# Second norm's modulations as rows in four quarters of the array, and the context's scale and shift on VectorE

## What is computed

```python
mod = silu(c) @ w_mod + b_mod                 # 6 x 1024, one for the context, one for the latent tokens
sh1, sc1, g1, sh2, sc2, g2 = split(mod, 6)
h = rmsnorm(x, norm1_g) * (1 + sc1) + sh1     # first norm
x = x + g1 * (mixer(h) @ w_o)                 # products "wo"
h = rmsnorm(x, norm2_g) * (1 + sc2) + sh2     # second norm
q = h @ wq                                    # products "wq"
x = x + g2 * peer(q, h)                       # expert retrieval over 16384 experts
y = rmsnorm(x, final_g)
```

## Time and profile before

| | us |
|---|---|
| median of 3 runs | 2236.38 |
| lowest and highest | 2235.76, 2242.87 |
| the profiled execution | 2240.45 |
| its span in the profile | 2238.6 |
| PE busy | 2134.1 (95%) |
| DVE busy | 1626.6 (73%) |
| ACT busy | 803.9 (36%) |
| POOL busy | 730.7 (33%) |

### The profile page before, as it was taken

How to read it: one execution, slowest core, us unless ns; L and a number is a source line. 1 busy time by engine, 2 the same in 40 slices (tenths; PEclk the granted TensorE clock), 3 DMA queues, 4 the chain that set the end, 5 groups by cost and what they waited for, 6 DMA issues and landing times.

```text
span 2238.6 us, 34858 instructions
## 1 busy us (share of the span) xinstructions
PE 2134.1 (95%) x11692; PEld 1903.6 (85%) x11692; DVE 1626.6 (73%) x3320; ACT 803.9 (36%) x1054; POOL 730.7 (33%) x524
## 2 busy tenths in 40 slices
PE   5889998799999999999699999999999999999998
PEld 1789998799999888888588889888888888888887
DVE  4448998242458679677988878887777777777777
ACT  1435554222332322222245545554223322332232
POOL 1123331332122476777422222121222223322331
PEclk8999999899699999999899999999999999999998
DMA  9212112334522488888567777676998999899893
GB/s 361 85 52 66 58 60 84 135 132 151 171 65 67 130 281 282 281 282 280 191 238 287 279 280 278 252 287 234 309 319 308 311 313 356 303 322 311 309 337 121
DMA packets 167472, 502.02 MB, mean 224 GB/s; under 512 B 16608, under 2 KB 74336, under 8 KB 165600
## 3 DMA queue, kind: packets, MB, share of 16 engines
q1 hardware_dynamic: 101872, 273.96, 35.7%
q0 software_dynamic: 46080, 167.79, 21.6%
q10 hardware_dynamic: 19440, 59.25, 6.7%
HBM read 436.45 MB, written 64.50 MB: 224 GB/s over the span
## 4 chain that ended last, share of the span: by engine, by line
PE 74%; issue 11%; DVE 5%; POOL 4%; DMA 3%; ACT 2%; SPq 0%; POOLq 0%; ACTq 0%; DVEq 0%
PE P L843 30%; PE P L550 21%; PE P L754 14%; PE P L778 4%; POOL rows L489 2%; POOL rowsX L489 1%; DMA gel_scratch<-gel 1%; PE P L658 1%; PE P L568 1%; DMA tb<-in_posT 1%; PE P L719 1%; DVE gq L1362 1%; DVE rstd L1240 1%; PE P L582 1%; ACT hs L867 0%
## 5 line engine op out<-in xcount | busy, mean ns | idle before, releaser
L867 ACT ACTIVATE wHi<-raw 128x1024 fp32r<-128x1024 f32 x330 | 346.2, 1049 | 1219.0 <-PE P L843 459.4
L754 PE MATMUL P<-hHi,wHi 128*128 128x480 f32 x1024 | 396.1, 387 | 20.5 <-POOL wLo L473 17.8
L754 PE MATMUL P<-hHi,wLo 128*128 128x480 f32 x1024 | 391.4, 382 | 0.0
L754 PE MATMUL P<-hLo,wHi 128*128 128x480 f32 x1024 | 389.4, 380 | 0.0
L1621 DVE TENSOR_TENSOR wLo<-raw,wHi 128x1024 fp32r<-128x1024 f32 x188 | 230.4, 1225 | 167.0 <-ACT wHi L867 164.8
L467 POOL TENSOR_TENSOR wLo<-raw,wHi 128x1024 fp32r<-128x1024 f32 (+1 forms) x76 | 187.1, 2463 | 491.0 <-ACT wHi L867 490.9
L489 POOL DMA_INDIRECT rows<-in_v_tab,Eg x160 | 176.1, 1101 | 468.1 <-DVE accB L1669 226.2
L550 PE MATMUL P<-hHi,wHi 128*128 128x320 f32 x960 | 230.0, 321 | 15.9 <-DVE hLo L1210 9.0
L754 PEld LDWEIGHTS P<-hHi,wHi 128*128 128x128 f32 x1024 | 193.8, 189 | 49.0 <-POOL wLo L473 18.2
L550 PE MATMUL P<-hLo,wHi 128*128 128x320 f32 x960 | 221.6, 312 | 0.0
L550 PE MATMUL P<-hHi,wLo 128*128 128x320 f32 x960 | 221.2, 312 | 0.0
(11 more groups left out here) (251 smaller groups left out, 3804.9 us busy)
## 6 DMA issues: line engine op xcount, KB each, us to landing
raw<-in_ublk SPq DMA_DIRECT2D x128, 512.0 KB, 4.2
raw<-in_v_tab SPq DMA_DIRECT2D x128, 512.0 KB, 6.0
raw<-in_wblk SPq DMA_DIRECT2D x104, 512.0 KB, 4.2
gel_scratch<-gel ACTq DMA_DIRECT2D x128, 240.0 KB
gsr<-gel_scratch SPq DMA_DIRECT2D x128, 240.0 KB, 5.9
gate_scratch<-stage ACTq DMA_DIRECT2D x6, 4096.0 KB, 15.0
gates4a<-gate_scratch SPq DMA_DIRECT2D x16, 768.0 KB, 7.5
gates4b<-gate_scratch SPq DMA_DIRECT2D x16, 768.0 KB, 8.2
```

The source lines that it names most:

```text
L754: last = nc.tensor.matmul(P[0][:, j % 2, 0:TD], w_[:, j % 2, k * 128:(k + 1) * 128], x_[:, k, C0:T], start=(k == 0 and a == 0 and b == 0), ...
L867: return nc.scalar.activation(out, in_, f, **kw)
```

## The change

Blocks 40 to 47 take the second form too. PE does block 40 and 41 ahead of the second norm's sums, once DVE has read the last product wo out of PSUM, with the parts in bank P[1]; blocks 42 to 47 follow the sums, and each one's turn stands just ahead of the next block's parts. ACT copies rows 40 and 41 ahead of its square root, rows 42 to 45 behind it, and rows 46 and 47 behind the first two slices of the norm. The wait for mrow_ready ahead of the sums goes; PE waits for mod_read and for the eviction of wo 7 there instead.

In both norms the scale and shift of the context's 128 columns goes from ACT to DVE, as one operation a slice behind the multiplication of the next slice; ACT waits for it (hA_ready) before it copies a slice to hHi. The loops over slices are written out.

```diff
-TURN = {m: n for n, m in enumerate(m for name, m in stream() if name == "mod" and 16 <= m < 40)}
+TURN = {m: n for n, m in enumerate(m for name, m in stream() if name == "mod" and m >= 16)}
+    def parts_of(m):
+        return P[2 if m < 40 else 1][:, TURN[m] % 2, 0:128]
...
-        pe.wait_ge(s["mrow_ready"], len(TURN))
+        pe.wait_ge(s["mod_read"], 1)
+        evicted(pe, "wo", KC - 1)
+        modulation_parts(40)
+        turn_parts()
+        modulation_parts(41)
+        modulation_turn(40)
         norm_sum(1)
-        turn_parts()
-        pe.wait_ge(s["mod_read"], 1)
-        for m in range(40, 48):
-            modulation(m)
+        for m in range(42, 48):
+            modulation_turn(m - 1)
+            modulation_parts(m)
+        modulation_turn(47)
         pe.wait_ge(s["keys_ld"], 16)
...
         def normed(n, scl, sh0):
+            if n:
+                mod_row(40)
+                mod_row(41)
             act.wait_ge(s["ms_ready"], n + 1)
             actf(rstd[:, :], rstd[:, :], ACT.Sqrt).then_inc(s["std_ready"], 1)
+            if n:
+                for m in range(42, 46):
+                    mod_row(m)
             act.wait_ge(s["mod_ready"], n + 1)
-            with act.Fori(0, KC) as k:
-                act.wait_ge(s["norm_t"], k + (n * KC + 1))
-                hk = hs[:, ds(k, 1), :].rearrange("p a n -> p (a n)")
-                for g, (c0, c1) in enumerate(((0, TA), (TA, T))):
-                    last = actf(hk[:, c0:c1], hk[:, c0:c1], ACT.Identity,
...
+            for k in range(KC):
+                act.wait_ge(s["norm_t"], n * KC + k + 1)
+                actf(hs[:, k, TA:T], hs[:, k, TA:T], ACT.Identity, scale=scl[:, k, 1:2], bias=mod[:, k + sh0, 1:2]
+                     ).then_inc(s["hF_ready"], 1)
+                act.wait_ge(s["hF_ready"], n * KC + k + 1)
+                act.wait_ge(s["hA_ready"], n * KC + k + 1)
+                actf(hHi[:, k, :], hs[:, k, :], ACT.Copy).then_inc(s["hi_ready"], 1)
+                if n and k < 2:
+                    mod_row(46 + k)
...
-        def normed(n):
-            with dve.Fori(0, KC) as k:
-                V.tensor_tensor(hs[:, ds(k, 1), :].rearrange("p a n -> p (a n)"),
-                                x[:, ds(k, 1), :].rearrange("p a n -> p (a n)"), rstd[:, :], ALU.mult
-                                ).then_inc(s["norm_t"], 1)
+        def normed(n, scl, sh0):
+
+            dve.wait_ge(s["mod_ready"], n + 1)
+            for k in range(KC + 1):
+                if k < KC:
+                    V.tensor_tensor(hs[:, k, :], x[:, k, :], rstd[:, :], ALU.mult).then_inc(s["norm_t"], 1)
+                if k:
+                    dve.wait_ge(s["norm_t"], n * KC + k)
+                    V.tensor_scalar(hs[:, k - 1, 0:TA], hs[:, k - 1, 0:TA], scl[:, k - 1, 0:1],
+                                    mod[:, k - 1 + sh0, 0:1], ALU.mult, ALU.add).then_inc(s["hA_ready"], 1)
```

More of the change, by code:

```diff
@@ L301, in build @@
     last_tiles = ((0, 0), (KS, 128 - KS), (C0, 0), (C0 + 128, 0), (384, KS), (512, 0))
-    names = ("x_ld x_pk x_up c_ld pos_ld small_ld keys_ld x_sv x_re tb_ready x_ready ones_ready csig_ready c_ready sq_done sq_used ms_ready std_ready norm_t "
+    names = ("x_ld x_pk x_up c_ld pos_ld small_ld keys_ld x_sv x_re tb_ready x_ready ones_ready csig_ready c_ready sq_done sq_used ms_ready std_ready norm_t hA_ready "
              "hF_ready hi_ready lo_ready prod_done xpp_ready pooled_ready poolmm_done py_ready sp_e sp_ready "
@@ L561, in norm_sum @@
             last.then_inc(s["sum_done"], 1)
[L563 to L570, removed]
         def modulation_parts(m):
@@ L581, in modulation_parts @@
                     k = a + j
-                    last = nc.tensor.matmul(P[2][32 * j:32 * j + 32, b % 2, 0:128], c32[:, k, :],
+                    last = nc.tensor.matmul(parts_of(m)[32 * j:32 * j + 32, :], c32[:, k, :],
                                             raw[:, n % RAW, k * 128:(k + 1) * 128], start=(a == 0), stop=(a > 0),
@@ L680, in modulations @@
             for n in after(name, m):
[L681 to L685, removed]
+                modulation_parts(n)
+                unturned.append(n)
         for m in range(2, 6):
@@ L867, in actf, with mod_row @@
             return nc.scalar.activation(out, in_, f, **kw)
+        def mod_row(n):
+            used(act, "mod", n)
+            if TURN[n] >= 2:
+                act.wait_ge(s["mod_tr"], TURN[n] - 1)
+            actf(mrow[:, TURN[n] % 2, :], parts_of(n), ACT.Copy).then_inc(s["mrow_ready"], 1)
         def mod_rows(name, m):
             for n in after(name, m):
[L871 to L874, removed]
+                mod_row(n)
         def squares(n):
@@ L1213, in mods @@
         def mods(m0, cnt):
-            if m0 in (16, 30):
+            if m0:
                 dve.wait_ge(s["mod_tr"], m0 + cnt - 16)
-            elif m0:
-                used(dve, "mod", m0 + cnt - 1)
             else:
@@ L1298, in _ @@
         scale(scl1, 8, V_N1, s["mod_ready"])
-        normed(0)
+        normed(0, scl1, 0)
         los(S_H1, KC, hLo, hHi, hs)
@@ L1445, in _ @@
         scale(scl2, 32, V_N2, s["mod_ready"])
-        normed(1)
+        normed(1, scl2, 24)
         los(S_H2, KC, hLo, hHi, hs)
```

## The result

| | before | changed |
|---|---|---|
| median of 5 runs, us | 2238.31 | 2225.66 |
| lowest and highest | 2235.76, 2242.87 | 2223.36, 2228.19 |
| span of the profiled execution | 2238.6 | 2223.9 |

The ratio is 0.9943, with a 95% interval of 0.9930 to 0.9955: 12.7 us faster, where 9.8 were forecast, and inside the range. In two more groups of runs the changed kernel was 9.5 and 12.5 us faster (see the experiments).

A forecast was written before the change was run, and what follows sets the result against it. Wq 0 was taken as held by PE's queue, with 27.31 us of modulations, and by the norm. Second norm 9.4 plus first norm 0.4 gave 9.8 us: 2226.6 against the median 2236.38, range 2221 to 2234.5.

The forecast's parts named there:

- The bound and the block: Ahead of wq 0: PE's queue, with 27.31 us of modulations 40 to 47, and the norm hold it; room 11.4 us.
- Sums behind block 41: Second norm: the sums wait for block 41's load, landing 5.1 us after issue; cost 2.3 us, bounds 0.7 to 3.2.
- Rows on ACT: Second norm: row copies, some 1.9 us a block with turn and next modulation, cost ACT 0.2 us and the chain none.
- DVE's eight operations: Context's scale and shift on DVE: eight operations at 0.26 us add 2.1 us to its loop, bounds 1.2 to 2.7.
- Wq 0: Second norm's first product: starts at 591.9, takes 9.4 us (8.96 to 9.9) with half clock first, ends at 601.3.
- the 9.4 forecast for the second norm: Second norm: wq 0 ends at 601.3 instead of 610.7, a gain of 9.4 us, bounds 7.4 to 12.3.
- What the move to DVE brings: Second norm: ACT's slice falls from 1.96 to 1.56 us without the context's part, leaving ACT 1.8 us to spare.
- First norm: First product starts 2.1 us later and ends at 82.3, bound by PE; gain 0.4 us, from -0.8 to 1.2.
- The rest: Stages behind both norms: same work in the same order, so the gain of 9.8 us passes on whole.
- The rivals: Half the gain, about 5 us (0.20); slower, about 2243, clock staying low (0.06); sums not delayed, about 2224 (0.04).
- the sums are not delayed: Rival: block 41 lands early and the clock rises in under 4 us; gain 12 to 13, 2224 us; chance 0.04.

The follow-up runs named there:

- scale and shift only: Kernel before the change, with the context's scale and shift moved to DVE in both norms, modulations 40 to 47 left as they were: 2237.55 us, ratio 0.9999.
- rows only: Changed kernel with scale and shift of both norms back on ACT, its loop still written out: 2225.71 us, ratio 0.9951.
- Old form, new places: Changed kernel with modulations 40 to 47 in their old form (weight block loaded, two columns run through) at their new places: 2233.21 us, ratio 0.9975.
- One ahead: Changed kernel with only modulation 40 ahead of the second norm's sums and block 41 behind them: 2225.44 us, ratio 0.9942.
- The repetition with 9.5 us: Changed kernel run again without edit, in the first group of follow-up runs: 2227.94 us against 2237.40 before, ratio 0.9956.
- written out: Kernel before the change with only ACT's loop over the eight slices of a norm written out: 2237.16 us, ratio 0.9996.
- early low halves: Changed kernel with DVE making each low half two slices behind its multiplication, both norms: 2222.31 us; with block 41 also behind the sums, 2222.65 in five rounds.

## Why the prediction was right, and where not

**The bound and the block.** Right. The block of 27.31 us on PE was what held wq 0; "scale and shift only" leaves it and gains nothing, "rows only" removes it and gains everything. "Old form, new places" shows that it is the form that counts: six blocks in the old form cost 20.27 us, in the new one a step of 2.05 each beside the norm.

**Sums behind block 41.** The mechanism is right, the size was too large: 2.3 us forecast, 1.1 measured (+6.01 against +4.89), inside the bounds of 0.7 to 3.2. The term that was too large is the landing. I took 5.1 us from issue because the neighbour took 6.0; the load was issued at 564.81,

```profile
564.81 0.80 SPq L396 DMA_DIRECT2D raw<-in_wblk  x2
```

and PE began at 568.65, so it was there within 3.8 (block 41's is the first of the two issues). Other executions of the same order have +6.33 and +6.65. "One ahead" takes the wait away and brings the start forward by 1.2.

**Rows on ACT.** Right: the exchange takes 2.05 us a block where 1.9 was forecast, and ACT came to its first slice 0.36 us behind the earliest time instead of 0.2. The rows 46 and 47 wait 0.3 us each. One term of the 1.9 was read wrongly: the 0.42 us of the earlier trace rows are one turn, recorded as two instructions, and not two turns of 0.21. In the changed kernel PE begins the next parts 0.49 us behind the start of a turn; the hand-overs, 0.2 instead of 0.3, make up for a part of it.

**DVE's eight operations.** Right: 0.26 each (580.47 to 580.72 and on), the loop 8.0 us, and from the first multiplication to the start of wq 0 8.9 us, where 9.0 was forecast.

**Wq 0.** 9.01 us where 9.4 was taken, within 8.96 to 9.9; the two other executions had 9.51 and 8.81. The term is one of chance: of the three executions of the changed kernel one had wq 0 at half clock for 3.9 us, one for 4.9 and one for 3.4, and "one ahead" for 6.1. Together with block 41's 1.2 us this is all of the difference between the 9.4 forecast for the second norm and the 11.0 in the first profile.

**What the move to DVE brings.** Here the working was right in the numbers and misleading in what it suggested. By it ACT had 1.8 us to spare, and I never worked out the change without the move. "Rows only" shows that it makes no difference: with the work on ACT, wq 0 starts 2 us earlier, since DVE's loop is shorter, and then waits for ACT's slices; with it on DVE it starts later and never waits. Both end at +32.7 to +33.1. My expectation of 3 to 4 us for that run was a miss. Two sizes were wrong in it: the slice of 1.86 (writing out the loop takes 0.09 off each, which I had not counted; with the move the slice took 1.48 and not 1.56) and the room between slices into which rows 46 and 47 fit.

**First norm.** 0.4 forecast with -0.8 to 1.2. Measured 1.2, 0.1 and 1.3 in three executions. The mechanism is as forecast: the first product starts 8.9 us behind DVE's first multiplication (72.76 in the changed kernel) and then runs without a wait. What it takes hangs on the clock. I took 9.4 us, with 4.7 at the half clock; it was 3.5, 6.0 and 3.4 us, which gives the 1.2, 0.1 and 1.3. A written-out loop alone gives 0.9, so the move itself adds 0.3 at best and takes 0.8 away when the clock rises late.

**The rest.** "I let the gain pass on whole" holds for the stages between, which repeat to 0.02 us (126.04 and 669.33), but the search and the tail move by 4 and 3 us in the same program, and the clock has a part in both. The second execution of the changed kernel against the first, at the same place of the search, first the slow one:

```profile
1105.40:1108.70 3.30, 3.30 (x10) 2.77 (x9) 3.30 (x7) 0.00 (x0) 2.69 (x3) 0.50 0.97 386
1303.40:1306.60 3.20, 3.20 (x12) 2.99 (x13) 3.20 (x7) 1.65 (x2) 1.14 (x1) 0.50 0.08 26
```

```profile
1104.40:1107.70 3.30, 3.30 (x19) 2.92 (x18) 3.30 (x9) 0.28 (x1) 2.75 (x3) 1.00 0.99 397
1302.40:1305.60 3.20, 3.20 (x17) 2.75 (x16) 3.20 (x11) 0.00 (x0) 0.60 (x1) 1.00 0.72 247
```

In the slow one the clock drops twice where it stays up in the other. Whether this causes all of the 4.2 us, or itself follows from a gap, was not tested. A drop alone does not cost so much: "written out" has a granted clock of 0.50 from 1310.9 to 1314.1 as well, with a search of 809.80. In the tail the same 48 instructions of the last norm (line 808) take 8.46 us in the first profile and 5.54 in the third:

```profile
2200.89 8.46 PE L808 MATMUL P<-ones,hs 128*128 128x2 f32 x48
```

```profile
2200.80 5.54 PE L808 MATMUL P<-ones,hs 128*128 128x2 f32 x48
```

From 2203.0 to 2205.8 the granted clock is 0.50 in the first profile and 1.00 in the third, so the tail's 2.9 us are the clock's.

So of the 3 us by which the runs beat the forecast, 1.6 belong to block 41 and wq 0, up to 0.8 to the first norm, and the rest cannot be told from such scatter. The repetition with 9.5 us did not beat it at all, so how close the number came is in part luck.

**The rivals.** None of their mechanisms came. By its size the gain of 12.7 is that of "the sums are not delayed" (more than 12, to which I gave 0.04), but the sums were delayed, by 1.1 us; my bounds of 7 to 12 had left out how far the search and the tail move. The clock rose within wq 0 in every kernel of the study, at the latest 6.1 us in. That ACT's copies would become the bound, which the Trainium skill, "TensorEngine Tiling (Array Packing)", section "PSUM Bottleneck", points to, is not seen in the changed kernel. In the ones with early low halves wq 0 starts behind the last turn, but of an exchange of 2.05 us ACT's copy is 0.28; the most of it is PE's own parts and turn at the half clock.

## What to carry to other kernels

A product that waits slice by slice is held by whichever of two is later, its queue or its slices, and relieving the one that is not later gains nothing: here the offload to VectorE is worth nothing that can be measured until the low halves are made early, and then 3 us. Where two parts of a change serve the same wait, work out the sum with each one alone as well. Work that is moved ahead of a waiting instruction must have its own data there: a block whose load is issued only when the last one is used up holds what follows, here the sums, by 1.1 to 1.8 us, although its own work is 1.1.

## What the runs showed of the hardware

- Weight loads of 128 x 128 with two columns to follow, eight blocks for 27 us without a gap, leave TensorE at 1.2 GHz, and the clock rose 2.9 to 4.1 us into the product behind them. A stretch of 2.9 us with 2.7 busy, most of it float32 products of 320 columns, left it there too, and the clock rose 3.5 us into the product.
- The Trainium skill, "TensorE: Matmul & The Clock Gate", section "What's actually happening", says that the transition varies, by 500 ns to either side, with where the first matmul lands. The traces agree that it varies, and show more: 3.4, 3.9 and 4.9 us for the same instructions of wq 0, and 3.4, 3.5 and 6.0 us for those of the kernel's first product. No run here shows what it hangs on.
- The same 128 x 1024 modulation costs TensorE 3.4 us with the weight block loaded, 1.08 us at the same clock with the vectors loaded in four quarters, and 0.64 us at the full clock; to the latter two add a copy of 0.28 us on ScalarE and a turn of about 0.5 us at the half clock.
- A ScalarE loop of three activations costs 1.95 us a turn as a loop and 1.86 us written out.
- Stages that repeat to 0.02 us stand beside stages that scatter by 3 to 4 us in one program, so a change of 2 us is better judged by positions counted from a common event than by the median of five runs.
